# Head outputs read back as quarter rows and turned by VectorE, in an encoder layer

## The reference

```python
def trunk(...):                                     # per layer, DEPTH = 1
    z = jnp.matmul(rmsnorm(x, norm1_g[l]), w_in[l])
    u, gates = z[..., :256], z[..., o5:]            # pool features, gates
    q, k, v, o = ...                                # 4 heads of 192 each
    y_pool = pool_mixer(u, pool_w[l], pool_scale[l])
    y_mlstm = mlstm_mixer(q, k, v, o, gates, gate_b[l], mh_norm_g[l])
    x = x + jnp.matmul(jnp.concatenate([y_pool, y_mlstm], axis=-1), w_out[l])
    x = x + expert_choice_ffn(rmsnorm(x, norm2_g[l]), w_router[l], w_gate[l], w_up[l], w_down[l])
    return rmsnorm(x, final_g)[:, N_META:]

def expert_choice_ffn(h, w_router, w_gate, w_up, w_down):
    aff = jax.nn.softmax(jnp.matmul(t, w_router), axis=-1)
    gate, idx = lax.top_k(aff.T, cap)               # each expert takes its best tokens
    ...                                             # SwiGLU of the taken tokens, added back
```

## Time and profile before

| | us |
|---|---|
| median of 3 runs | 1692.7 (1691.97 to 1693.19) |
| the profiled execution | 1695.98 |
| its span, first to last instruction | 1694.2 |
| TensorE busy | 1659.0 (98%) |
| VectorE / ScalarE / POOL busy | 505.2 / 404.4 / 503.7 |
| mean granted TensorE clock | 0.992 of full speed |

### The profile page before, as it was taken

How to read it: one execution, slowest core, us unless ns; L and a number is a source line. 1 busy time by engine, 2 the same in 40 slices (tenths; PEclk the granted TensorE clock), 3 DMA queues, 4 the chain that set the end, 5 groups by cost and what they waited for, 6 DMA issues and landing times.

```text
span 1694.2 us, 25780 instructions
## 1 busy us (share of the span) xinstructions
PE 1659.0 (98%) x10397; PEld 1428.2 (84%) x10397; DVE 505.2 (30%) x1111; ACT 404.4 (24%) x926; POOL 503.7 (30%) x465
## 2 busy tenths in 40 slices
PE   9999999999999999999999999999999999999996
PEld 6556698865799874455999999999999999999996
DVE  5575344663322660079211101111011110111105
ACT  3335134322221544455010011101111011110115
POOL 0073132631230454343131323312332223322220
PEclk9999999999999999999999999999999999999998
DMA  9311112311110636534587788877878779787794
GB/s 301 90 53 38 38 38 81 91 64 65 40 32 9 204 91 209 165 106 158 178 288 266 236 269 261 302 253 235 286 241 316 241 233 297 243 310 234 234 320 195
DMA packets 189812, 309.83 MB, mean 183 GB/s; under 512 B 12644, under 2 KB 77972, under 8 KB 189616
## 3 DMA queue, kind: packets, MB, share of 16 engines
q1 hardware_dynamic: 171840, 283.30, 48.5%
q0 software_dynamic: 17904, 25.62, 7.5%
HBM read 275.82 MB, written 33.07 MB: 182 GB/s over the span
## 4 chain that ended last, share of the span: by engine, by line
PE 90%; DVE 6%; ACT 2%; issue 1%; POOL 0%; DVEq 0%; ACTq 0%; POOLq 0%
PE bank L2470 33%; PE bank L2487 16%; PE bank L2183 8%; PE bank L2210 8%; PE bank L2374 5%; PE bank L2103 3%; PE bank L2139 2%; PE bank L2231 2%; PE bank L2304 2%; PE bank L2285 1%; DVE arena L1872 1%; DVE arena L1870 1%; DVE arena L1874 1%; PE bank L2149 1%; PE bank L2147 1%; PE bank L2507 1%
## 5 line engine op out<-in xcount | busy, mean ns | idle before, releaser
L2470 PE MATMUL bank<-arena 128*128 128x164 f32 x4096 | 573.0, 303 | 0.5 <-DVE arena L1979 0.5
L2470 PEld LDWEIGHTS bank<-arena 128*128 128x128 f32 x4096 | 570.8, 190 | 0.7 <-DVE arena L1979 0.7
L2487 PE MATMUL bank<-arena 128*128 128x164 f32 x1920 | 269.7, 303 | 0.0
L2487 PEld LDWEIGHTS bank<-arena 128*128 128x128 f32 x1920 | 268.0, 190 | 0.0
L973 POOL DMA_INDIRECT residual<-arena,cur_scatter x90 | 140.7, 1563 | 180.0 <-ACT arena L1452 157.2
L1989 DVE TENSOR_TENSOR arena<-bank,arena 128x328 f32<-128x328 f32 x64 | 32.0, 500 | 527.5 <-ACT arena L1441 517.7
L2183 PE MATMUL bank<-arena 128*128 128x400 f32 (+1 forms) x560 | 165.1, 458 | 6.7 <-ACT arena L1014 6.7
L2183 PEld LDWEIGHTS bank<-arena 128*128 128x128 f32 x560 | 110.0, 197 | 61.3 <-ACT arena L1014 8.6
L2374 PE MATMUL bank<-arena 128*128 128x512 f32 x320 | 146.1, 599 | 0.8 <-issue 0.7
L1441 ACT ACTIVATE arena<-bank 128x328 f32<-128x328 f32 x64 | 28.4, 444 | 480.5 <-PE bank L2470 480.5
L2210 PE MATMUL bank<-arena 128*128 128x192 f32 x840 | 137.7, 326 | 0.2 <-ACT arena L1014 0.2
(11 more groups left out here) (277 smaller groups left out, 1600.3 us busy)
## 6 DMA issues: line engine op xcount, KB each, us to landing
arena<-in_w_up SPq DMA_DIRECT2D x32, 2048.0 KB, 13.4
arena<-in_w_down SPq DMA_DIRECT2D x32, 2048.0 KB, 10.5
arena<-in_w_gate SPq DMA_DIRECT2D x32, 2048.0 KB, 7.8
arena<-in_w_in SPq DMA_DIRECT2D x7, 1536.0 KB, 7.3
arena<-in_x_sample SPq DMA_DIRECT2D x14, 512.0 KB, 6.0
arena<-x_features_first SPq DMA_DIRECT2D x11, 512.0 KB, 8.4
arena<-decay_rows SPq DMA_DIRECT2D x22, 256.0 KB, 4.8
arena<-state_rows SPq DMA_DIRECT2D x44, 128.0 KB, 4.2
```

The lines of the kernel that those rows point to most:

```text
L2470: last = pe.matmul(ps[2 * w + fp % 2][:, a * SLOTS:(a + 1) * SLOTS], ring[2 * (fp // 2) + w][:, k, f * P:(f + 1) * P], xeT[:, k, 0:SLOTS], ...
L2487: last = pe.matmul(result_tiles(4 + dp % 2)[:, a, 0:SLOTS], ring[4 + dp // 2][:, k, dt * P:(dt + 1) * P], hidT[:, k, :], start=k == 0, sto ...
```

## The change

Head features reach `yT_t` in another way, and in another order of features.

- Feature order. Of each pair's 384 features, partition p of block k now holds feature 3p + k, not 128k + p. The output weights are loaded to match: `"(p k) n -> p k n"` for each pair's 384 rows, three DMAs instead of one.
- First pair. `load_y` loads a tile of 128 tokens x 384 features with four DMAs: quarter q of the partitions gets features 96q to 96q + 95 of all 128 tokens, in four pieces of 96 features (384 bytes) on each partition. VectorE then transposes 32x32 blocks (`turn_y`): one instruction per pair, 128x384, its source read with a step of three elements.
- Second pair. Steps 0, 1 and 2 (HELD = 3) stay on TensorE, three transposes of `og` each, and one ScalarE move (`mixer_tiles`). For steps 3 to 10 POOL's `normed_gate` runs for all eight tiles ahead of the first `add`; SyncE stores each to `y1_d`, waits until all eight have landed, and from then on `load_y` brings eight quarter DMAs per step and `turn_y` has two instructions.
- Where `turn_y` stands on VectorE: call 0 in the last head tile, call 1 behind it, calls 2 to 7 ahead of the softmax, call 8 after five ranking rounds, call 9 after ten, call 10 after twelve.
- `mixer_ready(n)` on TensorE waits for `turn_y(n)` ahead of `project(n, 0)`.
- The semaphores `gb_in` and `prow_in` become one (`vectors_in`, waited for at 96), as do `carry_out` and `carry_in` (`carry_moved`); these lines are left out below, and so is the unchanged code between.

```diff
@@ -68,6 +68,8 @@
 RING_F = 3
+HELD = 3
+HEAD_TILES = 3
@@ -115,10 +117,10 @@
     mixed_keys = len(keys)
-    keys += [("yT", 0, 0), ("yT", 0, 1)]
+    keys += [("yT", 0)]
     for n in range(NT):
         normed = [("tT", n - 1, 0), ("tT", n - 1, 1)] if n else []
-        mixer = [("yT", n + 1, 0), ("yT", n + 1, 1)] if n + 1 < NT else []
+        mixer = [("yT", n + 1)] if n + 1 < HELD else []
         parts, sums = ([("lp", n - 1)], [("lg", n - 1)]) if n else ([], [])
@@ -170,6 +172,7 @@
     y_d = nc.dram_tensor("mixer_out", (T, PAIR), F32, kind="Internal").ap()
+    y1_d = nc.dram_tensor("mixer_out_late", (T, PAIR), F32, kind="Internal").ap()
     pool_d = nc.dram_tensor("pool_features", (2 * P, T), F32, kind="Internal").ap()
@@ -373,16 +376,13 @@
         EARLY = NT - 3
-        HELD = 3
         def slab(n, at=11 * D):
...
         x_t = [area("W", D, shift=2 * Y_W + s * D) for s in range(2)]
+        y1_t = [area("W", PAIR, shift=2 * Y_W + 2 * D + s * PAIR) for s in range(2)]
         yT_t, x2, t_t, tT_t = ([slab(2 * n + s) for s in range(2)] for n in range(4))
@@ -417,6 +417,7 @@
         y_in = [sem("y_in0"), sem("y_in1")]
+        y1_out, y_turned = sem("y1_out"), sem("y_turned")
         x3_in = [sem("x3_in0"), sem("x3_in1")]
@@ -444,12 +445,19 @@
+        def y_count(n):
+            return 16 * sum(5 + 4 * (a >= HELD) for a in range(n % 2, n + 1, 2))
         def load_y(sp, n):
-            i = ORDER_B[n]
+            rows = slice(ORDER_B[n] * P, ORDER_B[n] * P + P)
             if n >= 2:
-                multiplied(sp, ("yT", n - 2, 1))
-            sp.dma_start(y_t[n % 2][:, D_POOL:Y_W], y_d[i * P:(i + 1) * P, :]).then_inc(y_in[n % 2], 16)
+                sp.wait_ge(y_turned, n - 1)
+            for src, to in ((y_d, y_t[n % 2][:, D_POOL:Y_W]), (y1_d, y1_t[n % 2]))[0:1 + (n >= HELD)]:
+                quarters = src[rows, :].rearrange("(g t) (q f) -> q t g f", t=32, q=4)
+                for q in range(4):
+                    sp.dma_start(to[32 * q:32 * q + 32, :].rearrange("p (g f) -> p g f", g=4), quarters[q]).then_inc(y_in[n % 2], 16)
@@ -629,7 +637,10 @@
                     load_factors(NT + i)
-                sp.dma_start(wout, w_out[0].rearrange("(k p) n -> p k n", p=P)).then_inc(wout_in, 16)
+                sp.dma_start(wout[:, 0:2, :], w_out[0, 0:D_POOL].rearrange("(k p) n -> p k n", p=P)).then_inc(wout_in, 16)
+                for n in range(2):
+                    rows = slice(D_POOL + n * PAIR, D_POOL + n * PAIR + PAIR)
+                    sp.dma_start(wout[:, 2 + 3 * n:5 + 3 * n, :], w_out[0, rows].rearrange("(p k) n -> p k n", p=P)).then_inc(wout_in, 16)
                 sp.dma_start(g2b, g2[0:1, :].to_broadcast([P, D])).then_inc(g2_in, 16)
@@ -643,6 +654,11 @@
                     load_x3(sp, n)
+                for n in range(HELD, NT):
+                    i = ORDER_B[n]
+                    sp.wait_ge(y_scaled_b, n + 1)
+                    sp.dma_start(y1_d[i * P:(i + 1) * P, :], og[:, i, :, :].rearrange("p h d -> p (h d)")).then_inc(y1_out, 16)
+                sp.wait_ge(y1_out, 16 * (NT - HELD))
@@ -659,7 +675,7 @@
                     if n == NT - BT - 1:
-                        multiplied(sp, ("yT", n, 1))
+                        sp.wait_ge(y1_out, 16 * (NT - HELD))
                         load_expert(0)
@@ -924,12 +940,11 @@
                 st.do(pool.memset(small[:, 92:93], -1.0))
+                for m in range(HELD, NT):
+                    if ORDER_B[m] == EARLY:
+                        pool.wait_ge(rs_ready, 3)
+                    normed_gate(m)
                 for n in range(NT):
-                    m = n + HELD
-                    if m < NT:
-                        if ORDER_B[m] == EARLY:
-                            pool.wait_ge(rs_ready, 3)
-                        normed_gate(m)
                     add(n, 0)
@@ -1306,8 +1321,12 @@
                     for h in range(2):
-                        lo = D_POOL if name == "yT" and h == 0 else 512 * h
-                        move((name, n, h), slots[n % 2][:, lo:512 * h + 512], at=lo - 512 * h)
+                        move((name, n, h), slots[n % 2][:, 512 * h:512 * h + 512])
+                def mixer_tiles(n):
+                    if n < HELD:
+                        move(("yT", n), yT_t[n % 2][:, Y_W:D], w=PAIR)
@@ -1379,12 +1398,12 @@
-                halves("yT", 0, yT_t)
+                mixer_tiles(0)
                 last_norm(1)
...
                         take_sum(n, 0)
-                        halves("yT", n + 1, yT_t)
+                        mixer_tiles(n + 1)
                         halves("tT", n - 1, tT_t)
@@ -1647,6 +1666,17 @@
                         st.settle()
+                def turn_y(n):
+                    dve.wait_ge(y_in[n % 2], y_count(n))
+                    if n >= 2:
+                        multiplied(dve, ("wo", n - 2, 1))
+                    for c, src in ((D_POOL, y_t[n % 2][:, D_POOL:Y_W]), (Y_W, y1_t[n % 2]))[0:1 + (n >= HELD)]:
+                        st.do(dve.transpose(yT_t[n % 2][:, c:c + PAIR].rearrange("p (k g s) -> p g k s", k=HEAD_TILES, g=4),
+                                            src.rearrange("p (g s k) -> p g k s", g=4, k=HEAD_TILES)))
+                    st.settle()
+                    dve.sem_inc(y_turned, 1)
@@ -1806,6 +1836,8 @@
                             update_state(Cf, Cf, ("cf0", p, i), ("cf1", p, i), p, 0, i)
+                        if p and i == NT - 1:
+                            turn_y(0)
                         dve.wait_ge(own_full[m % 2], m // 2 + 1)
@@ -1838,6 +1870,8 @@
                             clear_borders(border)
+                    else:
+                        turn_y(1)
                     dve.wait_ge(rms_ready, 2 * p + 1)
@@ -1929,11 +1963,19 @@
+                for n in range(2, STEP_A + 2):
+                    turn_y(n)
                 softmax_first(0, STEP_A - 1)
...
                     read_out(dve, ("af", g))
-                rank(0, 0, rounds - 4)
+                rank(0, 0, 5)
+                turn_y(STEP_A + 2)
+                rank(0, 5, 10)
+                turn_y(STEP_A + 3)
+                rank(0, 10, rounds - 5)
+                turn_y(STEP_A + 4)
+                rank(0, rounds - 5, rounds - 4)
                 softmax_first(1, STEP_B - 1)
@@ -2319,15 +2361,25 @@
                         b = bank((name, n, h))
-                        for k in range(D_POOL // P if name == "yT" and h == 0 else 0, 4):
+                        for k in range(4):
                             last = pe.transpose(ps[b][:, k * P:(k + 1) * P], source(4 * h + k), ident[:, :])
...
                 def transpose_y(n):
-                    pe.wait_ge(y_in[n % 2], 32 * (n // 2 + 1))
+                    if n >= HELD:
+                        return
                     pe.wait_ge(y_scaled_b, n + 1)
+                    b = bank(("yT", n))
                     own = og[:, ORDER_B[n], :, :].rearrange("p h d -> p (h d)")
-                    transposes("yT", n, lambda k: y_t[n % 2][:, k * P:(k + 1) * P] if k * P < Y_W else own[:, k * P - Y_W:(k + 1) * P - Y_W])
+                    for k in range(HEAD_TILES):
+                        last = pe.transpose(ps[b][:, k * P:(k + 1) * P], own[:, k:PAIR:HEAD_TILES], ident[:, :])
+                    last.then_inc(full[b], 1)
+                def mixer_ready(n):
+                    pe.wait_ge(y_turned, n + 1)
+                    if n < HELD:
+                        read_out(pe, ("yT", n))
@@ -2409,9 +2461,9 @@
                 transpose_y(0)
-                pe.wait_ge(wout_in, 16)
+                pe.wait_ge(wout_in, 48)
                 for n in range(NT - 1):
-                    read_out(pe, ("yT", n, 1))
+                    mixer_ready(n)
                     if n == SHORT:
```

More of the change, by code:

```diff
@@ L288, in encoder_program @@
         params_in = sem("params_in")
-        prow_in, gb_in = sem("prow_in"), sem("gb_in")
+        vectors_in = sem("vectors_in")
         pool_par_in, mhg_in = sem("pool_par_in"), sem("mhg_in")
@@ L308, in encoder_program @@
         own_full, own_free = [sem("own0_full"), sem("own1_full")], [sem("own0_free"), sem("own1_free")]
-        carry_out, carry_in = sem("carry_out"), sem("carry_in")
+        carry_moved = sem("carry_moved")
         decay_in = [sem(f"decay{s}_in") for s in range(RING_E)]
@@ L571, in _ @@
                         sp.dma_start(gb[d * BW:d * BW + 4, what:what + 1],
[L572 removed]
+                                     gate_b[0, 2 * what + d:2 * what + d + 1, :].rearrange("a h -> h a")).then_inc(vectors_in, 16)
                 for i in ORDER_X[6:]:
                     load_x(i)
[L575 to L576 removed]
+                sp.dma_start(prow[0:36, :], conv_w[0].rearrange("k (c p) -> (k c) p", p=P)).then_inc(vectors_in, 16)
+                sp.dma_start(prow[36:48, :], conv_b[0].rearrange("(c p) -> c p", p=P)).then_inc(vectors_in, 16)
                 load_w(1)
@@ L608, in _ @@
```

(10 more changed lines are left out.)

5 lines of the change are left out of this document (1 added, 4 removed).

## The result

| | before | after |
|---|---|---|
| median, 11 runs each, us | 1692.32 (1689.09 to 1695.14) | 1697.23 (1695.47 to 1702.05) |
| profiled execution / its span, us | 1695.98 / 1694.2 | 1698.71 / 1696.9 |
| TensorE busy / VectorE busy, us | 1659.0 / 505.2 | 1651.9 / 520.8 |

Ratio 1.0032, 95% interval 1.002 to 1.0044: slower by 3.4 to 7.4 us, on a forecast of 1697.3. The page says what was exchanged for what: TensorE 7.1 us less busy, VectorE 15.6 more, and nearly twice as many small packets (23572 under 512 B, where there were 12644).

A forecast was written before the change was run, and what follows sets the result against it. The chain was taken to run through TensorE's out projection to the softmax, then VectorE's ranking rounds. -3.85 + 3.4 + 5.0 = +4.55, called +4.6, on the median of 1692.7 gave 1697.3 us; range 1691.4 to 1702.0.

The forecast's parts named there:

- TensorE's saving: Transposes dropped from TensorE ahead of the softmax: the first ranking round was to start 3.85 us earlier.
- The calls in the rounds: Calls 8, 9 and 10 on VectorE between ranking rounds, two transposes each, paid in full: 3.4 us.
- Both bounds: Limits for the three calls between ranking rounds: 2.7 us at 0.45 each, about 6.9 if each takes twice as long.
- rival 2: Strided transposes on VectorE take twice as long, 6.9 us for three calls, the wait stays: 1700.8 us, chance 0.13.
- The wait before call 10: VectorE stands before call 10 until tile 10's loads land: 5.0 us, bounds 3.3 and 9.8.
- the loop: Call 9 releases projection 9, then tile 7's logits, scale and store, then tile 10's loads behind it: 10.3 us in all.
- The hole of TensorE: TensorE stands 5 us before projection 9 until call 9 ends, costing nothing by itself; its clock may fall.
- At the last half: Sum of the terms at the last half of the residual sum on VectorE: -3.85 + 3.4 + 5.0 = +4.55 us.
- The covers: Slack for other moved steps, put at nothing: 2.3 us before projection 2, 1.7 at the fourth head tile's product.
- rival 4: Store and reload of tile 2 take 6 us more, 3.7 beyond the cover, whole saving gone: 1701.0 us, chance 0.05.
- rival 1: Not slower: tile 10 has landed when call 10 comes, sum -0.45 us: 1692.2 us, chance 0.20.
- rival 3: Faster: neither calls nor wait lie on the chain, all 3.85 us come through: 1688.9 us, chance 0.07.

The follow-up runs named there:

- call 10 late: Changed kernel with call 10 moved from behind the twelfth ranking round to behind the fourteenth and the second softmax; 1694.28 us, ratio 1.0011 to the kernel before.
- hole alone: Kernel with tiles 8 to 10 transposed on TensorE, no calls between rounds, projection 9 held until VectorE's eleventh round is done; 1694.48 us, ratio 1.0007 to before.
- late tiles on TensorE: Changed kernel with tiles 8 to 10 loaded in whole rows and transposed on TensorE, their three calls gone; 1690.11 us, ratio 0.9983 to the kernel before.
- first pair alone: Changed kernel with only the first pair by quarter loads and VectorE, the second pair on TensorE for all eleven tiles; 1694.58 us, ratio 1.0012 to before.
- tile 10's loads ahead: Changed kernel with tile 10's nine loads issued on SyncE's queue ahead of the store of tile 7's normed rows; 1694.61 us, ratio 1.0011 to before.
- call 9 early: Changed kernel with call 9 after eight ranking rounds instead of ten, nothing else changed; 1692.3 us, ratio 0.9999 to the kernel before.
- late tiles again: Second run of the same kernel as late tiles on TensorE, nothing changed; 1691.2 us, ratio 0.9981 to the kernel before.

## Why the forecast held, step by step

The sum of +4.6 us met what was measured, and the wait of call 10, its largest term, has the cause that the prediction gave. That 1697.3 met 1697.23 is luck in that closeness: the difference of the medians is 4.9, the ratio gives 5.4, the stages of the traces 3.5, and errors named below cancelled each other.

**TensorE's saving** was put at 3.85 and is 3.78, in every run of the whole change within 0.02. Three strided transposes take 0.34 (630.93 to 631.27), the 0.11 each that the sum used, so their step costs TensorE nothing.

**The calls in the rounds** were put at 3.4 and take 4.30 (1.45 + 1.42 + 1.43). This is the term that was mis-sized: I took a value between the two rows for a straight source where the step adds 131 ns to each of six. Both bounds held. The Trainium skill ("Advanced Engine Details and Errata", Memory Cachelines) asks for two hits on each 16-byte line and gives no price for fewer; up to twice the straight 559 was my estimate from it. The trace has 1.23 times, so rival 2, which rested on a doubling, is off.

**The wait before call 10** was put at 5.0 and is 4.99. The parts were each close: the way from projection 9 to the logits 2.36 where 1.25 and 0.9 for the clock stood, the store 1.52 for 1.5, the issues 0.52 each for 0.48, the landing 2.35 for 3.2. The issues' excess of 0.3 and the logits' 0.2 were made good by the landing. The 5.0 itself stood between 4.5 at full clock and 5.4 at half clock; the clock did fall, so by the prediction's own sum the wait was to be 5.4. That it came out to 0.01 is chance; that the loop is its cause is shown, by three runs that cut it at call 9, at the loads and at call 10. By the median, the quarter loads in pieces of 384 B landed 2.6 (first pair) and 2.0 us (second) after their issue, the whole rows before 3.4. So the rule of the Trainium skill on transfers under 512 B ("DMA: Bandwidth & Descriptors", Specifications), by which I put the wait nearer its upper bound, had no effect here that a row shows.

**The hole of TensorE** was forecast with 5 us, its end with call 9 and its clock at half: 5.53, released by L1679, granted clock 0.50. What I said of it, that by itself it costs nothing, is true only under cover of the wait for the loads: without that cover it cost 2.08 (call 10 late), and without calls too 5.9 (hole alone). The link missing in my chain is that the second softmax needs the logits as well as the loads do. It didn't change the sum, since the two waits run side by side.

**At the last half** the sum was +4.55. The trace has -3.78 + 4.30 + 4.99 = +5.51, and 0.66 less for a row that nobody looked at: the product of the second softmax took 0.87 before (at 771.22) and takes 0.21 at 775.96. The traces point to POOL. In the kernel before, one of POOL's additions (`add`) is under way when the product starts:

```profile
770.93 1.09 POOL L895 TENSOR_TENSOR arena<-arena 128x512 f32<-128x512 f32 x1 [3.99 <-ACT arena L1346]
...
771.22 0.87 DVE L1851 TENSOR_TENSOR arena<-arena,smx 128x48 f32<-128x48 f32 x1
```

The addition ends at 772.02 and the product 0.07 behind it. In both traces of late tiles on TensorE (0.90) and in first pair alone (0.38) it is the same, with 0.06 to 0.07 from end to end. In the other six traces, hole alone among them, no addition is under way when the product starts, and it takes 0.21. No run moved the addition by itself. With the 0.66 the sum is +4.85, and T1 minus A is +4.80.

**The covers** held. Tile 2 is turned at 639.2, earlier than the 646.3 that I gave, since stores and loads landed faster than at the median. I also misread where projection 2 starts. The row at 649.63 is the rest of tile 1's second half, behind the logits of tile 0; in the changed kernel that is this row, and projection 2 begins behind 14 of its 22 records, near 654.1:

```profile
647.99 9.69 PE L2426 MATMUL bank<-arena 128*128 128x512 f32 x22
```

The cover is then some 15 us, and 8.5 by the prediction's own times, where it said 2.3, so rival 4 was never near. Of calls 2 to 7 none ends later than its projection needs: TensorE has no pause of over 0.5 us from 624 to 754. Call 10 waited, which rules out rival 1, and the three calls were paid in full, which rules out rival 3.

**Behind the last half** I had no term, and there the trace has one, -1.34 us (T1 to T2), which the last section describes. With it the traces say +3.5 and the medians +4.9, with 3.4 to 7.4 in the interval. In the timed runs the ratio lies above the sum of the stages in all eight measurements: by 1.9 here, 2.2 with tile 10's loads ahead, 1.4 with call 10 late and 0.3 to 0.8 in the other five. Each single difference is within its interval, but all go one way. The granted clocks of the timed executions point to TensorE's clock: with call 9 early their mean is 0.9930, and 0.9943 for the kernel before beside them, about 2 us of the span, while from A on the trace of the one lacks as much of full clock as that of the other (4 us stretches as in the last section: 6.8 and 6.9). Whether the more falls ahead of A, or the gain behind the last half is rarer in executions without a profile, stays open.

## What to carry to other kernels

Work that is moved from a busy engine to an idle one is free only where the idle engine isn't on the chain at that moment: eight of the eleven tiles were turned at no cost, the three that fell between ranking rounds cost more than all eleven saved. When loads stand behind a store on one queue, ask what the store waits for; here a call two rounds earlier took 5 us of waiting away, and 4 of them came through. And when a wait is removed, look for what it covered: the second-latest thing is in the trace of no kernel until the latest is gone.

## What the runs showed of the hardware

**Where a spell at half clock stood, a later one is missing.** Between the last half and the gather, TensorE runs 44 matmuls on the identity that only keep it busy, and the gathered rows' transposes stand behind them. The 44 in the kernel before, in the changed kernel and in the run with the hole alone:

```profile
812.42 6.81 PE L2357 MATMUL bank<-ident 128*128 128x128 f32 x44
...
814.00:816.00 2.00, 2.00 (x11) 0.50 0.57 121
```

```profile
816.50 5.18 PE L2409 MATMUL bank<-ident 128*128 128x128 f32 x44
...
818.00:820.00 2.00, 2.00 (x20) 1.00 0.57 94
```

```profile
814.67 5.18 PE L2429 MATMUL bank<-ident 128*128 128x128 f32 x44
...
816.00:818.00 2.00, 2.00 (x20) 1.00 0.42 76
```

They took 6.80 to 6.81 with the granted clock at 0.50 in part of them in the kernel before and in both runs with the late tiles on TensorE, and 5.18 at 1.00 in the changed kernel and with the hole alone. TensorE's last pauses ahead of them, 0.75 and 0.64, are the same in all. The hole alone has neither calls nor late loads; what it shares with the changed kernel is the hole, which lies between 755 and 762 in both, and the fall of the clock there. So the earlier spell, not the calls, goes with the missing later one; that is seven traces (5.18 in each) against three, and why is not shown. Nor does the length of a pause alone decide whether the clock falls: it fell at 1.68 us in the head stage and at 3.63, 4.23 and 5.5 here, and not at the 2.81 before 779.69, behind which no stretch has less than 1.00. The same pause of the same work can go either way. This is the one of rows 9 with call 9 early:

```profile
342.99 1.58 PE L2346 MATMUL bank<-arena 128*128 128x193 f32 x8 [1.68 <-DVE arena L1836]
...
344.00:348.00 4.00, 4.00 (x18) 1.00 0.33 114
```

Eight matmuls that took 2.25 us in the kernel before take 1.58 here.

**Where executions differ.** The start of the last eight head matmuls lies between 617.29 and 622.08 in the ten traces. The spells at half clock account for all but about 1 us of it. Two of the kernel before and the same stretches with call 9 early (A at 622.02 and 617.29):

```profile
192.00:196.00 4.00, 4.00 (x10) 0.57 0.01 4
...
388.00:392.00 4.00, 4.00 (x9) 0.50 0.02 4
```

```profile
192.00:196.00 4.00, 4.00 (x15) 1.00 0.02 4
...
388.00:392.00 4.00, 4.00 (x15) 0.95 0.00 0
```

Adding up 4 us times what the clock lacks of 1 over all such stretches from 60 us on gives 6.8 and 1.7, and A less that is 615.2 and 615.6. Over the ten traces it is 615.2 to 616.4, and the three that have the same spells (before, late tiles again, hole alone) agree in A itself to 0.06 us. The last two carry the change's edits ahead of A, the two more loads of output weights among them, so these cost nothing. A difference of a few microseconds between two profiled executions says nothing until both are cut where they have the same work.
